# The order of side work in a two-layer hybrid mixer kernel, rewritten: triangular solve, output tail and first dense products

## The reference, cut to what matters

```
proj = hn @ w_in
o_gdn = gated_delta_rule(...)     # 6 heads, chunks of 64, a unit triangular solve
o_dsw = dilated_window_attention  # 6 heads: softmax over 3 window patterns
o_sb  = stick_breaking(...)       # 4 heads: exp(log_sigmoid(z) + suffix sum of log_keep)
h = h + concat(rms_norm of each) @ w_out
h = h + swiglu(rms_norm(h))       # layer 0; layer 1: mixture of experts
h = h + (p @ ple_proj) * sigmoid(rms_norm(h) @ ple_gate)
```

## Time and profile before

| | |
|---|---|
| time, median of 3 (lowest, highest) | 1599.09 us (1597.61, 1600.72) |
| the profiled execution's own time, its span | 1600.72 us, 1598.9 us |
| PE busy | 1564.8 us, 98% of the span |
| DVE, ACT, POOL busy | 1270.4 us (79%), 1031.2 us (64%), 169.6 us (11%) |
| mean granted clock of PE | 0.993 |
| PE's share of the chain that ended last | 96% |
| first layer's solve and tail | about 109 to 174 us |
| second layer's solve and tail | about 490 to 554 us |

### The profile page before, as it was taken

One profiled execution on the slowest core, in us unless ns is written; L12 is line 12 of the kernel. 1 busy time (PEld: TensorE's weight loads), 2 busy tenths in 40 slices (PEclk: granted clock), 3 DMA queues, 4 the chain that ended last, 5 costly groups with the idle time before them and its releaser, 6 DMA issues.

```text
span 1598.9 us, 22790 instructions
## 1 busy us (share of the span) xinstructions
PE 1564.8 (98%) x8476; PEld 1334.9 (83%) x8476; DVE 1270.4 (79%) x1198; ACT 1031.2 (64%) x992; POOL 169.6 (11%) x199
## 2 busy tenths in 40 slices
PE   7999999999999979999999999999999999999997
PEld 7999999998999768888888888888888888887876
DVE  5977655657877768888888888888888888888985
ACT  6575533436648357777767777776776776776774
POOL 2561100000374020000000000000001000001000
PEclk9999999999999989999999999999999999999999
DMA  8560654455544359999999999999999999999991
GB/s 323 197 205 28 227 214 178 174 214 198 179 145 135 126 160 388 374 365 383 367 362 382 367 364 390 361 361 390 362 356 392 365 358 391 366 356 396 375 348 46
DMA packets 84622, 466.50 MB, mean 292 GB/s; under 512 B 16848, under 2 KB 26448, under 8 KB 30544
## 3 DMA queue, kind: packets, MB, share of 16 engines
q1 hardware_dynamic: 80528, 450.93, 74.7%
q0 software_dynamic: 4032, 14.71, 2.5%
HBM read 453.66 MB, written 11.95 MB: 291 GB/s over the span
## 4 chain that ended last, share of the span: by engine, by line
PE 96%; DMA 1%; ACT 1%; DVE 1%; issue 1%; SPq 0%; DVEq 0%; POOLq 0%; POOL 0%; ACTq 0%
PE ps L2006 21%; PE ps L2010 21%; PE ps L2007 21%; PE ps L1999 8%; PE ps L2001 7%; PE ps L2000 7%; PE ps L2445 2%; PE ps L2153 1%; PE ps L2247 1%; PE ps L2162 1%; DMA raw<-in_experts 1%; PE ps L2108 1%; PE ps L1979 1%; PE ps L2407 0%; PE ps L2418 0%
## 5 line engine op out<-in xcount | busy, mean ns | idle before, releaser
L708 DVE TENSOR_TENSOR wlo<-raw,whi 128x2048 fp32r<-128x2048 f32 x421 | 949.5, 2298 | 102.1 <-ACT whi L704 100.7
L704 ACT CAST whi<-raw 128x2048 fp32r<-128x2048 f32 x421 | 785.7, 1917 | 66.4 <-DMA raw<-in_experts 66.4
L2006 PE MATMUL ps<-whi,xh 128*128 128x512 f32 (+3 forms) x1504 | 597.6, 398 | 10.6 <-ACT whi L704 6.6
L2007 PE MATMUL ps<-whi,xl 128*128 128x512 f32 (+3 forms) x1504 | 584.1, 389 | 0.0
L2010 PE MATMUL ps<-wlo,xh 128*128 128x512 f32 (+3 forms) x1504 | 405.5, 391 | 0.2 <-DVE wlo L708 0.2
L2006 PEld LDWEIGHTS ps<-whi,xh 128*128 128x128 f32 x1504 | 284.1, 189 | 78.2 <-ACT whi L704 7.9
L2010 PEld LDWEIGHTS ps<-wlo,xh 128*128 128x128 f32 x1504 | 280.9, 188 | 64.7 <-DVE wlo L708 0.6
L2007 PEld LDWEIGHTS ps<-whi,xl 128*128 128x128 f32 x1504 | 284.3, 189 | 57.2
L1999 PE MATMUL ps<-xh,whi 128*128 128x256 f32 x656 | 187.4, 286 | 0.0
L2000 PE MATMUL ps<-xl,whi 128*128 128x256 f32 x656 | 186.0, 284 | 0.0
L2001 PE MATMUL ps<-xh,wlo 128*128 128x256 f32 x656 | 186.0, 284 | 0.0
(11 more groups left out here) (334 smaller groups left out, 1342.9 us busy)
## 6 DMA issues: line engine op xcount, KB each, us to landing
raw<-in_experts SPq DMA_DIRECT2D x336, 1024.0 KB, 4.9
raw<-in_stream SPq DMA_DIRECT2D x85, 1024.0 KB, 5.3
y_rows<-work POOLq DMA_DIRECT2D x7, 512.0 KB, 5.1
y_rows<-work POOLq DMA_DIRECT2D x1, 2560.0 KB, 10.5
m_rows<-work SPq DMA_DIRECT2D x2, 768.0 KB, 4.1
work<-x_inv_rows SPq DMA_DIRECT2D x2, 768.0 KB, 5.3
work<-xt_rows SPq DMA_DIRECT2D x2, 768.0 KB, 7.0
cst<-in_consts SPq DMA_DIRECT2D x1, 1127.5 KB, 12.7
```

The lines of the kernel that those rows point to most:

```text
L704: nc.scalar.copy(whi[:, n % RING, :], raw[:, n % RING, :]).then_inc(s_hi, 1)
L708: nc.vector.tensor_tensor(wlo[:, n % RING, :], raw[:, n % RING, :], whi[:, n % RING, :].bitcast(F32), ALU.subtract).then_inc(s_lo, 1)
L2006: pe.matmul(out, xu, wu, start=start, stop=False)
L2007: return pe.matmul(out, xd, wu, start=False, stop=False)
```

## The change

It gives `ASIDE` other places, with effect on all engines: E, F and the squares spread to level 5, the logarithm goes from place 3 to 4, softplus from 7 to 6 and 7, the suffix sums from all four at 11 to one each at 8 to 11, the gate from 6 to 9, the two splits of ACT from 7 and 10 to 2 and 6. ACT makes the stick-breaking exp(-|z|) and the first three window exponentials ahead of level 4. DVE makes one split inside the solve that it made behind it. PE makes `W0` ahead of the transposes `OT` 0 and 1 and moves three output products. ACT's roots and splits of the tail swap places. In the dense part the second side of the first two feed-forward tiles is no longer begun early, which also makes the start and stop flags plain. Behind the tables the diff shows ACT's program, then DVE's, then PE's.

```diff
-ASIDE = (("exp", (-1, -1, -1, 0, 0, 0)), ("E", (0, 0, 1, 2, 2, 3)), ("F", (1, 1, 2, 3, 3, 3)), ("log1p", (3,)),
-         ("squares", (3,)), ("gate", (6,)), ("softplus", (7, 7, 7, 7)), ("scales", (8,)), ("CS", (11, 11, 11, 11)),
-         ("splits", (7, 10)))
+ASIDE = (("exp", (-1, -1, -1, 0, 0, 0)), ("E", (0, 0, 1, 2, 3, 4)), ("F", (1, 1, 2, 3, 4, 5)), ("log1p", (4,)),
+         ("squares", (5,)), ("softplus", (6, 6, 7, 7)), ("CS", (8, 9, 10, 11)), ("scales", (8,)), ("gate", (9,)),
+         ("splits", (2, 6)))
...
-    for key, who in (("OT", 0), ("OT", 1), ("W0", "v"), ("S", "a"), ("KS0", "v"), ("KS1", "v"), ("U", "a"), ("QS0", "a"),
+    for key, who in (("W0", "v"), ("OT", 0), ("OT", 1), ("S", "a"), ("KS0", "v"), ("KS1", "v"), ("U", "a"), ("QS0", "a"),
...
-                    elif kind == "CS" and k < HS - 1:
+                    elif kind == "CS":
                         grown(k)
...
                 split.ahead(1)
-                beside("exp", 0)
+                drained(act, ("Z", L, HS - 1), "a")
+                for j in range(2):
+                    ins = nc.scalar.activation(es_pair(L, j), es_pair(L, j), ACT.Exp, scale=-1.0)
+                ins.then_inc(st.sem, st.up())
+                for k in range(3):
+                    beside("exp", k)
                 token_major(L, 2)
+                act.wait_ge(st.sem, st.n)
...
-                        if lev == SMALL and g == GS // 2:
-                            beside("exp", 1)
...
-                    if lev == SMALL:
-                        beside("exp", 2)
...
-                        if lev == SMALL and g == 0:
-                            drained(act, ("Z", L, HS - 1), "a")
-                            for j in range(2):
-                                ins = nc.scalar.activation(es_pair(L, j), es_pair(L, j), ACT.Exp, scale=-1.0)
-                            ins.then_inc(st.sem, st.up())
...
                 turned_output(1)
-                grown(HS - 1)
...
-                head_roots(2)
+                split.ahead(1)
                 filled(act, ("O0", L))
                 nc.scalar.copy(o[:, 0, 0:DG], bank(("O0", L), 0, DG)).then_inc(s_free["a"], 1)
+                head_roots(2)
                 split.ahead(1)
-                turned_output(4)
                 head_roots(1)
-                split.ahead(1)
-                turned_output(2)
-                turned_output(3)
+                for c in (4, 2, 3):
+                    turned_output(c)
...
-                        if k == 2:
-                            causal(0)
+                        if k > 1:
+                            causal(k - 2)
+                    elif kind == "splits" and k == 0:
+                        split.ahead(1)
...
-                turned_output(L, 0)
-                turned_output(L, 1)
                 filled(dve, ("W0", L))
...
-                for k in range(1, HS):
-                    causal(k)
-                split.ahead(1)
+                causal(2)
+                causal(3)
+                turned_output(L, 0)
+                turned_output(L, 1)
...
-                turned_output(L, 4)
                 v, _ = head_columns(1)
                 nc.vector.tensor_tensor(v, v, zt[:, :, :], ALU.mult).then_inc(st.sem, st.up())
+                turned_output(L, 4)
...
+                heads_of(("W0", L), lambda: (drained_y(), pe.wait_ge(s_vt, NB * L + 1)), system(xt, 0),
+                         lambda k: vt[:, 0, HD * k:HD * k + HD])
                 turned_output(0)
                 turned_output(1)
-                heads_of(("W0", L), lambda: (drained_y(), pe.wait_ge(s_vt, NB * L + 1)), system(xt, 0),
-                         lambda k: vt[:, 0, HD * k:HD * k + HD])
-                output_products(0, 0)
                 heads_of(("S", L), lambda: drained(pe, ("W0", L), "v"), lambda k: kd[:, HD * k:HD * k + HD],
                          lambda k: vn[:, 0, HD * k:HD * k + HD],
-                output_products(0, 1)
+                output_products(0, 0)
...
                 with_state("QS", 0)
+                output_products(0, 1)
...
                 output_products(0, 6, 7)
+                output_products(1, 6)
                 turned_output(2)
                 turned_output(3)
-                output_products(1, 6, 7)
+                output_products(1, 7)
...
-                                  x_part(T * k, T), k == 0 and (side == 0 or f >= 2),
-                                  k == KC - 1 and (side == 1 or f >= 2))
+                                  x_part(T * k, T), k == 0, k == KC - 1)
...
                     turned_residual(1, LATE)
-                dense_up(f, 1, early)
...
-                dense_up(f, 1, range(KC) if f >= 2 else late).then_inc(s_fill, 1)
+                dense_up(f, 1, range(KC)).then_inc(s_fill, 1)
```

More of the change, by code:

```diff
@@ L1120, in beside @@
                     elif kind == "log1p":
-                        act.wait_ge(st.sem, st.n)
                         for j in range(2):
```

## The result

The changed kernel is slower: 1623.86 us (median of 4 runs, 1619.82 to 1633.3) against 1598.35 us (median of 4, 1597.39 to 1600.72) for the kernel before. The ratio is 1.0165, with a 95% interval of 1.0129 to 1.0201, so about 25.5 us. The forecast was 1615, the range ended at 1622. The profiled execution took 1623.08 us with a span of 1621.2, which is 22.3 more than the span before.

What follows compares the result with a forecast made beforehand. PE, busy 98% of the span, was taken as the bound. New waits of 8.45 us in the first layer and 7.4 in the second, 15.85 in all, on the median 1599.09 gave 1614.9, forecast 1615; range 1606 to 1622.

Steps and rivals of the forecast that it cites:

- 1, level 4's updates: Ahead of level 4's updates, PE waits 2.0 us for ACT's copy of `P`, delayed by exponentials moved in front.
- 2, level 6's last products: Before level 6's last product group, PE waits 1.1 us for DVE's subtraction, behind squares, reduction and softplus.
- 3, `W0`: Before `W0` in the last level, PE waits 1.25 us for DVE's chain of suffix sums, scales, gate and subtractions.
- 4, `S` and the first `w_out` product: After `W0`, PE waits 0.2 us for DVE's scaling, then 1.05 for `OT` 0's lower part; together 1.25 us.
- 5, `OT` 4: In the tail, PE waits 1.25 us before `OT` 4 for DVE's head scales behind ACT's later root.
- 6, residual: At the residual, PE has one chunk less to cover DVE's splits and adds and waits 0.55 us.
- 7, dense start: At the first layer's dense start, fewer matmuls cover the late transposes; PE waits 1.05 us for DVE.
- the clock falls in the new waits: Rival: new waits thin the work, so the clock falls; one 3.4 us stretch per layer gives 1622; chance 0.14.
- not slower: Rival: the second layer shifts and the clock fall at 440 goes, -3.4 us, 1595.7; chance 0.04.
- DVE catches up: Rival: waits from `W0` to `OT` 4 vanish because DVE and ACT have slack; time 1607.4, chance 0.15.
- No change: Rival: the waits are taken back later, behind the second tail where experts are chosen; chance 0.05.

Runs made afterwards that it cites:

- experiment 10: Only ACT's order of roots, splits and copies in the tail changed, against the kernel before: 1600.85 us, ratio 1.0022.
- experiment 2: The changed kernel with only ACT's exponentials ahead of level 4 put back as before: 1610.72 us, ratio 1.0079 to the kernel before.
- experiment 3: The kernel before with only the new side-work places in `ASIDE` and what hangs on them: 1605.74 us, ratio 1.0044.
- experiment 9: The kernel before with only the tail's new order (`W0` ahead of output transposes, moved output products, ACT's roots): 1615.0 us, ratio 1.0096.
- experiment 8: The kernel before with three needless ACT copies of 128x1536 ahead of the first layer's late transposes: 1600.17 us, ratio 1.0013.

## Why the prediction missed, point by point

**The direction and the walk were right.** The predicted waits and those of the profile after, first layer:

| part | predicted | measured | released by |
|---|---|---|---|
| 1, level 4's updates | 2.0 | 1.97 | ACT's copy of `P` |
| 2, level 6's last products | 1.1 | 1.04 | DVE's subtraction at 137.25 (below) |
| 3, `W0` | 1.25 | 1.45 | DVE's last subtraction, L1540 |
| 4, `S` and the first `w_out` product | 1.25 | 0.24 + 1.0 | DVE's scaling, then `OT` 0's lower part |
| 5, `OT` 4 | 1.25 | 1.48 | DVE behind ACT's root |
| 6, residual | 0.55 | 0.25 | DVE's residual adds |
| 7, dense start | 1.05 | 1.02 | DVE, L1342 |
| sum | 8.45 | 8.45 | |

The second layer has the same but the last, and its wait before the first `w_out` product is mostly hidden by the fall at 540, so the two-layer sum of 15.9 counts it at its first-layer size. The errors of single parts (up to 0.3) cancel; that the sums agree to the second digit is luck. DVE's timeline shows two of the links: its squares, reduction and softplus steps stand without a hole ahead of group 3's subtraction, and later the root holds it 2.71 us.

```profile
133.00 0.96 DVE L1592 TENSOR_TENSOR attn<-hn 128x768 f32<-128x768 f32 x1
...
137.25 0.35 DVE L1540 TENSOR_TENSOR work<-work,ps 128x192 f32<-128x192 f32 x1
...
163.12 0.20 DVE L1617 RECIPROCAL work<-work 128x8 f32<-128x8 f32 x1 [2.71 <-ACT work L1149]
```

The subtraction at 137.25 is group 3's; PE's last product group starts at 137.70, right behind it.

**The step that failed** is the clock. The forecast's sum has no term for it, and the range ends where its rival ends, at 1622. So what was wrong is the price and the weight of that rival: "the clock falls in the new waits", with "one more such stretch per layer gives 1615 + 6.8", at 0.14. It was priced from the only fall with a row, where 3.4 us of work were lost, and held unlikely because the same thin work kept full clock in the first layer. In the profiled execution the fall behind level 4 lasts 13.7 us in each layer and loses about twice as much. The ground for holding it unlikely was weak as well: the same work of the first layer had full clock in that execution, but in seven of twelve it has not. And the trace of before had the better row, a fall behind a wait, behind the second layer's tail (PE's timeline, then the window):

```profile
563.77 0.36 PE L2391 MATMUL ps<-work,cst 128*128 128x8 f32 x2 [2.95 <-DVE work L1839]
```

```profile
565.00:572.00 7.00, 5.71 (x28) 5.69 (x28) 5.49 (x8) 7.00 (x8) 0.00 (x0) 0.51 0.25 103
```

That waits are followed by falls could be read there before the change ran.

Now the size, by landmarks: from the first product of level 4 to the first transpose `T` it was 60.65 us before, in both layers; now it is 181.79 - 107.34 = 74.45 in the first and 74.99 in the second. That is 13.80 and 14.34 more, of which 7.4 are waits and 6.4 and 6.9 the clock. The two together are 28.1; the dense start adds 1.0, the absent fall near 442 gives back about 3.0, what lies before level 4 is 2.1 shorter, and from the last transposes on 1.8: 22.3, the difference of the spans but for rounding. The last three are not shown to come from the change. The clock's net part agrees with its mean over the span, 0.993 before and 0.987 after: 0.006 of 1621 is 9.7 us, about as much as the medians have beyond the waits.

**What would have been right:** the sum of the waits, 15.85, plus about ten: 1625. My rival had the place (behind a new wait, in thin work), half of the price, and far too small a chance. The rival "not slower" let the fall near 442 go; it is absent from this execution, by chance as far as the twelve profiles tell, and it did not decide.

**The other rivals.** "DVE catches up" fell: parts 3 to 5 measured 4.17 instead of 3.75. "No change" fell: from the last transposes to the end only 1.8 us came back. No version tried is measurably faster than the kernel before, whose solve and tail left PE no wait to remove.

**Part 5 and the table load.** In the profile after, ACT has:

```profile
161.00 0.48 ACT L1194 COPY hn<-ps 128x384 f32<-128x384 f32 x1 [1.35 <-PE ps L2242]
161.49 1.28 ACT L1149 ACT_TABLE_LOAD   x1
162.79 0.30 ACT L1149 ACTIVATE work<-work,cst 128x8 f32<-128x8 f32 x1
```

The load starts 0.01 us behind the copy's end, and the activation 1.30 us after the load's start. The drain of 1.38 us that the Trainium skill ("ScalarE: Activation LUTs", section "What ACT_TABLE_LOAD costs") adds to the load of 1.28 appears neither here nor in experiment 10; the measurement decides, and the load alone, which the sum took, was right. The 0.23 by which this wait is longer than forecast is not the table's: 0.15 of it is the hand-over from DVE (its scaling ends at 164.84) to PE (164.99), which the sum left out in this part.

**What stays open.** Why the fall behind one and the same wait lasts 3.4 us once and 17.1 the other time is not settled, nor what makes a long one begin behind a wait of 1.45 in one execution of experiment 2 and, by their times, not in the four others. Nor is it settled whether thin work behind a wait is needed for a long fall. The 29 executions of the changed kernel on record scatter between 1618.7 and 1635.1 us, and the time goes with the mean clock: 1619.82 at 0.990, 1633.3 at 0.979. Why the fall near 442 comes in one execution and not in another is not shown either.

## What to carry to other kernels

When side work is moved among engines and TensorE is the bound, walk the feeding engines forward and sum the waits; in the changed kernel that was good to 0.3 us for each wait, in experiment 3 it missed one of 0.7. Then look at each wait's size, and give the clock a term of its own in the sum: here two waits near 2 us with a long run of thin matmuls (64 and 128 columns) behind them cost 3.4 to 3.9 times their own length. For its price look in the trace for falls that stand behind waits. Waits of at most 1.5 us, thirteen in one kernel here, cost about their sum in four executions of five.

## What the runs showed of the hardware

- The granted clock fell to 1.2 GHz behind single waits of 1.9 to 2.1 us in the solve and tail, for 3.4 to 17.1 us while PE was busy with hardly a gap, and for 20.4 us behind 3.65 us. Behind 1.27 us at the same place it did not fall in the profiled execution.
- Behind waits of 1.45 to 1.5 us in the tail it fell for 17.1 us (experiment 2), for 3.4 us (second layer of the changed kernel, experiments 2 and 9) or not at all (experiment 10).
- Behind a wait of 2.2 us between matmuls of 256 columns (experiment 8) it fell for 3.4 us, as it did behind two of the waits of 2.0 to 2.1 us in the solve.
- The clock fell without any wait, too, behind 24 matmuls of two columns, in 13 of 24 cases.
- The cost beyond the waits is 9.6 and 12.3 us for two waits of 2.0 and of 2.1 us, and 19.5 for two of 3.65.
- The changed kernel's 29 executions differ by up to 1% (1618.7 to 1635.1 us), and the time goes with the mean clock (0.990 to 0.978). The 45 executions of the kernel before that were timed beside the experiments lie between 1593.5 and 1601.9 us, at 0.991 to 0.995.
